# Moving the skip-term loads, two state updates and the norm work in a diffusion backbone step

## The reference

```python
# layer 0: attention heads | bidirectional SSD heads -> output projection; layer 1: mLSTM -> output projection
def step(h, inp):                                  # ssd_scan, chunks of 128 tokens
    xc, dtc, Bc, Cc = inp
    cum = jnp.cumsum(dtc * A, axis=1)
    ...
    y = jnp.einsum('bijgr,bjgrp->bigrp', wts, xc)
    y = y + jnp.einsum('bign,bgrpn->bigrp', Cc, h) * jnp.exp(cum)[..., None]
    h = h * jnp.exp(cum[:, -1])[..., None, None] + jnp.einsum('bjgn,bjgr,bjgrp->bgrpn', Bc, w_end, xc)
    return h, y
y = y_f + flip(y_b) + d_skip * xs                  # the skip term
...
x = x + g * (y @ w_out)                            # output projection, gated residual
x = x + g2 * sqrelu_mlp(modulate(x, norm_ffn, sh2, sc2), w_ff1, w_ff2)
```

## Time and profile before

| what | value |
|---|---|
| median of 3 runs | 3481.57 us (3480.6 to 3484.84) |
| profiled execution | 3488.92 us, span 3487.2 us |
| granted PE clock, mean | 0.965 |
| PE busy | 3279.4 us, 94% |
| DVE, ACT, POOL busy | 56%, 29%, 15% |
| scan | 764 to 956 us |
| output products, layer 0 | 976 to 1168 us |
| output products, layer 1 | 2504 to 2642 us |

### The profile page before, as it was taken

One profiled execution on the slowest core, in us unless ns is written; L12 is line 12 of the kernel. 1 busy time (PEld: TensorE's weight loads), 2 busy tenths in 40 slices (PEclk: granted clock), 3 DMA queues, 4 the chain that ended last, 5 costly groups with the idle time before them and its releaser, 6 DMA issues. The chain is left out here.

```text
span 3487.2 us, 47687 instructions
## 1 busy us (share of the span) xinstructions
PE 3279.4 (94%) x18360; PEld 2888.6 (83%) x18360; DVE 1958.4 (56%) x3359; ACT 1000.2 (29%) x2033; POOL 533.8 (15%) x548
## 2 busy tenths in 40 slices
PE   7999999988878999999999799999979999999997
PEld 5665665655677999999999688888869999999996
DVE  5995551337766555445544676664456455445546
ACT  2223442335454311211121242222243111211121
POOL 0010100004443201110111003332222101110110
PEclk7999999999988999999999899999989999999998
DMA  6561111124173211111111212222241111111111
GB/s 264 217 268 42 36 51 40 53 73 112 42 238 94 61 43 37 48 42 42 36 48 42 85 33 63 64 65 67 76 133 49 43 43 36 48 42 42 36 49 55
DMA packets 189173, 257.94 MB, mean 74 GB/s; under 512 B 19580, under 2 KB 165220, under 8 KB 183260
## 3 DMA queue, kind: packets, MB, share of 16 engines
q1 hardware_dynamic: 189020, 255.86, 22.3%
HBM read 231.67 MB, written 24.15 MB: 73 GB/s over the span
## 5 line engine op out<-in xcount | busy, mean ns | idle before, releaser
L1863 PE MATMUL PS<-AHL,WH 128*128 128x384 f32 x3072 | 782.7, 335 | 6.0 <-DVE WL L2212 6.0
L1863 PE MATMUL PS<-Y,WH 128*128 128x384 f32 x3072 | 780.2, 334 | 3.1 <-issue 3.1
L2232 DVE SCALAR_TENSOR_TENSOR XT<-PS,MOD,XT 128x384 f32<-128x384 f32 (+2 forms) x1024 | 495.1, 514 | 224.1 <-PE PS L1863 223.5
L1863 PEld LDWEIGHTS PS<-AHL,WH 128*128 128x128 f32 x3072 | 557.3, 189 | 6.6 <-DVE WL L2212 6.6
L1863 PEld LDWEIGHTS PS<-Y,WH 128*128 128x128 f32 x3072 | 554.6, 188 | 4.2 <-issue 3.7
L1863 PE MATMUL PS<-AHL,WL 128*128 128x384 f32 x1536 | 514.6, 335 | 0.0
L1863 PE MATMUL PS<-Y,WL 128*128 128x384 f32 x1536 | 513.1, 334 | 0.0
L2219 DVE TENSOR_TENSOR AHL<-SQ,AHL 128x384 fp32r<-128x384 f32 x192 | 157.2, 819 | 430.7 <-ACT AHL L1968 430.7
L2146 POOL TENSOR_TENSOR SQ<-RT 128x384 f32<-128x384 f32 x192 | 179.8, 937 | 1319.5 <-ACT RT L1963 1300.1
L1957 ACT ACTIVATE WH<-WU 128x1024 fp32r<-128x1024 f32 x128 | 135.5, 1059 | 729.8 <-DMA WU<-in_wff 729.8
L608 PE MATMUL PS<-HT,WR 128*128 128x384 f32 x960 | 322.2, 493 | 14.9 <-PEq L531 10.3
(11 more groups left out here) (359 smaller groups left out, 4426.8 us busy)
## 6 DMA issues: line engine op xcount, KB each, us to landing
WU<-in_wff SPq DMA_DIRECT2D x128, 512.0 KB, 3.6
XT<-in_wmod SPq DMA_DIRECT2D x13, 2048.0 KB, 9.3
F<-in_wmod SPq DMA_DIRECT2D x9, 2048.0 KB, 9.2
OWR<-in_wslots SPq DMA_DIRECT2D x24, 768.0 KB, 5.1
WR<-in_wslots SPq DMA_DIRECT2D x8, 2048.0 KB, 8.6
PW<-in_wslots SPq DMA_DIRECT2D x24, 512.0 KB, 4.4
OWOR<-in_wslots SPq DMA_DIRECT2D x24, 512.0 KB, 4.3
EB<-cum_rows SPq DMA_DIRECT2D x36, 256.0 KB, 4.4
```

The costliest lines, as they stand in the source:

```text
L1863: mm = nc.tensor.matmul(out, wt(w), x, start=(n == 0 and i == 0), stop=(n == len(terms) - 1 and i == 2))
L2232: ins = nc.vector.scalar_tensor_tensor(out=x, in0=PS[:, 3 + j % 4, a - c * TC:e - c * TC], scalar=MOD[:, l, 40 + b, cond:cond + 1], in1=x, ...
```

## The change

Scan: skip third 0 is loaded right after pairs 0; pairs 1 and rows 1 then go ahead of `HS`; third 2 is loaded after pairs 3 and third 1 after pairs 4, each with a count of its own; DVE waits for them at n = 0, 3 and 6. Steps 16 and 17 no longer update their states: `carry`, `inputs`, `update` and `add_state` end at 15. Output products, both layers: the 24 operations of the first two thirds are listed by tile in `norm_at`; `mean` and `norm_root` move from b = 2 to b = 3, `square_sums` from after tile 8c + 1 to after 8c + 2. Layer 1: high part 6 is made at b = 5 and 7 at b = 6, and DVE makes low parts 6 and 7 ahead of the weights' low part.

```diff
         steps = [(0, 0), (1, 0)] + [x for t in range(8) for x in ((0, 1 + t), (1, 8 - t))]
         NS = len(steps)
+        NU = NS - 2
...
+                def skip_load(c):
+                    sp.dma_start(YL[c][:, :, :], skip_spill[:, c, :, :]).then_inc(skip_in[c].sem, 16)
+
                 rows_in(0)
                 pairs_in(0)
+                skip_load(0)
+                pairs_in(1)
+                rows_in(1)
                 for d in range(2):
                     sp.dma_start(HS[:, d, :], ssd0[:, d, :]).then_inc(state_in[d].sem, 16)
-                pairs_in(1)
-                rows_in(1)
                 pairs_in(2)
-                for c in range(NC):
-                    sp.dma_start(YL[c][:, :, :], skip_spill[:, c, :, :]).then_inc(skip_in[min(c, 1)].sem, 16)
                 for n in range(3, NS):
+                    if n == 4:
+                        skip_load(2)
+                    if n == 5:
+                        skip_load(1)
...
-                for n in range(NS):
-                    if n + 1 < NS:
+                for n in range(NU):
+                    if n + 1 < NU:
                         carry(n + 1)
-                    if n + 2 < NS:
+                    if n + 2 < NU:
                         inputs(n + 2)
...
-                    if n + 1 < NS:
+                    if n + 1 < NU:
                         update(n + 1)
...
-                    if n in (0, 3):
-                        dve.wait_ge(skip_in[n // 3].sem, skip_in[n // 3].at(16 + 16 * (n // 3)))
+                    if n in (0, 3, 6):
+                        c = {0: 0, 3: 2, 6: 1}[n]
+                        dve.wait_ge(skip_in[c].sem, skip_in[c].at(16))
...
+                    if n + 1 < NU:
                         add_state(n + 1)
...
+            norm_at = {(1, 4): (0, 2), (1, 5): (2, 4), (1, 6): (4, 6), (1, 7): (6, 8), (2, 0): (8, 11), (2, 1): (11, 14), (2, 2): (14, 16),
+                       (2, 4): (16, 18), (2, 5): (18, 20), (2, 6): (20, 22), (2, 7): (22, 24)}
...
-                        if n in (KD + 1, 2 * KD + 1):
+                        if n in (KD + 2, 2 * KD + 2):
                             square_sums(n // KD - 1)
...
-                        if l == 1 and c < 2 and b < 7:
-                            split_high(c + 1, b)
-                            if b == 6:
-                                split_high(c + 1, 7)
+                        if l == 1 and c < 2:
+                            for k in {5: (5, 6), 6: (7,), 7: ()}.get(b, (b,)):
+                                split_high(c + 1, k)
...
-                        if c >= 1 and b == 2:
+                        if c >= 1 and b == 3:
                             norm_root(act, c - 1, RB)
-                        if c >= 1 and 3 <= b <= 6:
-                            per = (first_op[c] - first_op[c - 1]) // 4
-                            for m in range(first_op[c - 1] + per * (b - 3), first_op[c - 1] + per * (b - 2)):
-                                high(m)
+                        for m in range(*norm_at.get((c, b), (0, 0))):
+                            high(m)
...
                         c, b = n // KD, n % KD
+                        if l == 1 and c < 2 and b == 7:
+                            split_low(c + 1, 6)
+                            split_low(c + 1, 7)
                         if n + NB - 1 < NW:
                             out_unit(n + NB - 1)
...
-                        if l == 1 and c < 2 and b == 7:
-                            split_low(c + 1, 6)
-                            split_low(c + 1, 7)
...
-                        if c >= 1 and b == 2:
+                        if c >= 1 and b == 3:
                             mean(c - 1)
-                        if c >= 1 and 3 <= b <= 6:
-                            per = (first_op[c] - first_op[c - 1]) // 4
-                            ops(first_op[c - 1] + per * (b - 3), first_op[c - 1] + per * (b - 2))
+                        if (c, b) in norm_at:
+                            ops(*norm_at[c, b])
```

More of the change, by code:

```diff
@@ L300, in hybrid_step @@
         mix_low, mix_low_pool = count("mix_low"), count("mix_low_pool")
-        yna_stored, skip_stored, skip_in = memory_loaded, loaded, [inter_spread[3], spilled]
+        yna_stored, skip_stored, skip_in = memory_loaded, loaded, [inter_spread[3], spilled, conv_done]
         skips_scaled, rows_taken, rows_split, zeros_ready = last_gated, gates_zero, gates_split, gates_high
@@ L1671, in hybrid_step @@
             inter_spread[n].close(32 * 6)
-        for n in range(2):
-            skip_in[n].close(16 + 16 * n)
-        for e, n in ((inter_ready, NS), (inter_scaled, NS), (inter_added, NS), (state_scaled, NS + 1), (state_added, 2 * NS)):
+        for c in range(NC):
+            skip_in[c].close(16)
+        for e, n in ((inter_ready, NS), (inter_scaled, NS), (inter_added, NS), (state_scaled, NU + 1), (state_added, 2 * NU)):
             e.close(n)
-        for e, n in ((x_scaled, NS), (state_read, NS), (weights_ready, 2 * NS), (chunk_summed, NS), (step_taken, NT),
-                     (update_summed, NS), (exp_ready, 16 * NS)):
+        for e, n in ((x_scaled, NU), (state_read, NS), (weights_ready, 2 * NS), (chunk_summed, NS), (step_taken, NT),
+                     (update_summed, NU), (exp_ready, 16 * NS)):
             e.close(n)
```

## The result

The changed kernel takes 3450.93 us (median of 4 runs, 3448.57 to 3455.5), the kernel before, beside it, 3483.2 us (4 runs): a ratio of 0.9907, 95% interval 0.9893 to 0.9921, 32.3 us faster. The forecast was 3452 us and 29.4 us off, so the sum held. The profiled execution took 3448.57 us.

A forecast was written before the change was run, and what follows sets the result against it. PE, busy 94% of the span, bounds the kernel, so only its idle or low-clock stretches give time back. 6.6+2+7.2+13.6 = 29.4 us off 3481.57 gave 3452 us, range 3438 to 3467.

The forecast's parts named there:

- Front of the scan: Scan start: reordering the skip thirds on the queue shortens PE's wait for rows; 6.6 us, between 3 and 11.
- The 9.3 us: Scan step 2: PE's product that waits for `cum_r` moves from 797.09 to 787.8, 9.3 us earlier.
- the charge of 3.8 us for the rows of step 4: Scan: rows of steps 3 and 4 land late behind skip thirds, so 3.8 us come back as new PE waits.
- End of the scan: Scan end: dropping the last two state updates shortens PE's and DVE's path; 2 us, between 0.5 and 3.
- PE's last 64 products follow it: Scan end: DVE's bank-freeing add comes about 1.9 us earlier, and PE's last 64 products follow it; 2 us.
- Layer 0: Layer 0 output products: spreading the first norm brings tile 16 forward; 7.2 us, bounds 3 and 10.6.
- the two named waits: Layer 0, before and in tile 16: PE's 2.89 us wait goes, the 7.76 us one falls to under 4.
- Layer 1: Layer 1 output products: spread norm and earlier low parts bring PE's last sum of squares forward 13.6 us; bounds 7 and 19.
- PE needs only 5 tiles x 4.24 after its sum at 2597, and stands still for about 1 us a tile: Layer 1, last third: DVE becomes the bound and PE idles about 1 us in each tile.
- Partial: Rival, chance 0.24: queues that work moves onto are dearer than charged; 17 us off, 3465 us.
- slower: Rival, chance 0.04: gaps in each tile hold PE at 1.2 GHz in the last thirds; 51 us slower, 3533 us.
- The signs: Scan and both layers: trace observations set beforehand as showing the forecast right or wrong, such as named waits shrinking.

The follow-up runs named there:

- combined: Changed kernel with layer 1's x reload behind one more weights load, DVE awaiting x only before its add, PE keeping the dropped updates' products: 3448.94 us, ratio 0.9886.
- weights_again: Changed kernel with layer 1's reload of x issued behind one more of the weights, timed a second time: 3441.75 us, ratio 0.9881.

## Why the prediction was right, step by step

- **Front of the scan: 6.6 forecast, 7.7 measured** (4.5 to 10.8), the right mechanism, and luck in the size. The 9.89 us wait went and PE's clock no longer fell behind it. Three of its terms were off. The 9.3 us stand on the longest wait of five (8.0 on average). The rows of step 1, put at "no change", cost 1.4 us more. And the charge of 3.8 us for the rows of step 4 was too high: PE waited 0.37 to 2.08 us, 1.4 on average. With the measured averages the term is 8.0 + 1.1 - 1.4 - 1.4 = 6.3 us, so the errors cancelled. For the charge, I had third 1 and those rows on the queue from 798.5; SP issued the third at 793.73 and the rows from 795.24 on. I also had the rows wait for the state output in front of them (2.4 us), and they did not: it was issued at 794.76 and took 9.1 us or more to land, so till 803.8, and PE used the first of the rows at 802.74. So the rule of the Trainium skill (DMA: Bandwidth & Descriptors, "Queues, rings and completion order"), by which a later small transfer may finish before an earlier wide one, is borne out for the state output. Behind the skip third it is not: that took 8.7 us from 793.73, so till 802.4, and in the eight kernels PE had the rows between 0.3 us before and 1.6 us after the third had landed.
- **End of the scan: 2 forecast, 0.6 or nothing measured.** The failed step is "PE's last 64 products follow it": DVE's add did come 2.3 us earlier (1.9 forecast), but PE then waited 3.90 us instead of 1.86 and 48 of those products took 4.5 to 5.1 us instead of 2.84. I had costed the removed PE work as a gain only. With the front, the two come to 8.6 us forecast and 6.6 to 8.6 by the stage table.
- **Layer 0: 7.2 forecast, 7.6 measured** by the table. The waits account for it: before and in tile 16 PE stood still for 11.6 us before and for 4.2 after, 7.4 less; 2.89 and 5.1 (7.76 less 2.67) of that are the two named waits, and a wait of 0.36 that is now 1.15 takes 0.8 back.
- **Layer 1: 13.6 forecast, 14.8 between the two profiles, 15.4 over all.** The wait before tile 16 was to be 6.6 us and is 6.14; from the reload of x to ACT's weights it was to take 11.2 us and took 11.21; DVE's last third was to take 36.6 us and took 35.8 (2569.95 to 2605.73, the end of its last add). These are the terms that carried the sum. The step that failed here is "PE needs only 5 tiles x 4.24 after its sum at 2597, and stands still for about 1 us a tile": PE did not stand still by the tile, it ran ahead and paid in one wait of 7.99 us at the end. That changes nothing in the 13.6 us, since DVE's last add sets the last sum either way. Of the 1 to 2 us that the forecast missed, the clock can hold all: it was given 2.7 us, and PE's time at the lower level in this stage fell from 37.5 us to 26.5 (17.0 to 22.9 in the three other kernels with all of the change).
- **The rivals.** "Partial" (17 us) lies outside the interval. For "slower" the point of decision was a granted clock below 0.73 in the last third. It was 1.00, but the rival was not put to the test: its condition, a short gap in each tile, did not come about. So these rows say nothing for or against the oscillation that the Trainium skill describes (TensorE: Matmul & The Clock Gate, "A second HAM failure mode: psum-queue depth-cycling").
- **The signs.** Of those for "right", two held only in part: the new `cum_r` wait was to be 1 to 4 us and is 0.56 here (1.4 in eight kernels on average), and "PE with gaps" in the last third did not happen. DVE's wait for the skip term, 2.20 us here, is 1.0 to 4.4 in the nine kernels with the new order, so above 3 in five of them.
- **Open.** It stays open why one kernel spends 27.3 us at the lower clock between the layers and another 37.5, when no edit touches that stretch. For the two kernels profiled twice it came out alike (1326.1 and 1326.4; 1323.1 and 1323.0). The 5 us are as large as the gains under discussion. The profiled execution of `combined` is 9.7 us longer than that of `weights_again`, and that does not come from layer 1 (0.3): 5.0 between the layers, 4.3 in the scan and 3.6 in the rest are longer, 0.8 in layer 0 and 2.7 ahead of the scan shorter.

## What to carry to other kernels

Read a small transfer's wait together with what was issued ahead of it on its queue: here 2 KB rows behind 4.6 MB cost PE 7 to 10 us, and issuing each large piece just before its use gave most of it back. A burst of work on an engine that lags before a deadline is worth spreading even where that engine becomes the bound later, provided that the waits next in line (here the sum of squares, one tile later) move with it. When several parts are tried, cut every profile at the same few rows: layer 0 repeated to within 0.8 us over nine kernels and layer 1 to within 1.4 over four, where the total needed differences of 5 us and more. And where a stage moves that no edit touches, add up its time at the lower clock before looking for another cause. Before pricing a lag as a gap in every tile, count how many tiles the waiting engine may run ahead: here it was three, and the lag came as one wait at the end.

## What the runs showed of the hardware that was not expected

- Work taken out of a wait cost clock here. With PE's gap at 3.90 us, 48 products of 128x128 took 4.5 to 5.1 us, in 7 of 7 executions; with a gap of 1.84 to 2.18 us they took 2.84 us in 5 of 7 and 4.34 and 5.39 in the other two.
- The same code took 1322.6 to 1328.2 us between the layers in fourteen profiled executions, with 27.3 to 37.5 us of it at the lower clock and 37 to 40 us of idle time on PE.
- Rows of 2 KB reached PE before a 0.5 MB transfer to memory issued ahead of them on the same queue had landed (802.74 against 803.8), but not clearly before a 1.5 MB load.
- DVE's two masks of step 16 took 4.05 us beside POOL's inputs and carries and 2.35 us without them, and leaving these out saved nothing that can be measured: 3483.92 against 3484.53 us.
